# First loads on one queue, products on ones before the data, V scaled per token, four low parts on GpSimd

## The chip, the cores and the metric

One NeuronCore of a Trainium2 chip runs the whole program. The time is device microseconds of that core; the median of three runs is given. TensorE is called PE in the profile, VectorE is DVE, ScalarE is ACT, GpSimd is POOL, and SP is the queue of SyncE, which here only issues transfers.

## What is computed

The reference runs two layers and then one sparse-attention block over 512 tokens of width 1024, in float32. A layer is:

```python
h = rmsnorm(x, norm_mix_g[l])
x = x + mixer_block(h, w_in[l], ...)      # mLSTM with input/forget gates, windowed attention, two gates, w_out
h = rmsnorm(x, norm_mlp_g[l])
x = x + jnp.square(jax.nn.relu(h @ w_up[l])) @ w_down[l]
```

Of the mixer only the beginning matters here: `proj = h @ w_in` gives among others the attention's keys `ak` and values `av` (256 columns each), the eight gate columns `mi` and `mf`, and the mLSTM's input. With `rs = 1/sqrt(mean(x*x) + eps)` per token, `h` is `x * gain * rs`, so a product of `x * gain` with the weights needs only to be multiplied by `rs` per token behind it. For the gates, `log_sigmoid(mf + b)` is summed over time and a running maximum is taken.

## The kernel before

Everything is transposed: tiles are 128 channels by 512 tokens, eight of them (`k` = 0 to 7) for the width. Each float32 operand of a large product is split into a high and a low part (`fp32r`), and a product is three matmuls: high*high, low*high, high*low. A weight unit is 1024x128: SP loads its raw form (512 KB), ScalarE writes its high part in two halves (L902), GpSimd its low part in two halves (L457, `split_pairs`), TensorE takes 24 matmuls of 512 columns (L497 to L499). Units alternate between two buffers; SP loads unit n+2 when both low halves of unit n are there, and ScalarE splits a half when TensorE is through with the one before it in that buffer.

The order of work of every engine is written out as a list of steps, and each engine walks through the same list in order: `u0, h0, m1, u1` are the four quarters of a unit. The change touches the list `PRE` that stands before the main loop of each layer:

- k0 and k1: products for the attention's keys, from `hx`, the raw `x*gain` split in high (ScalarE, L997) and low (VectorE, L1509).
- norm: ScalarE squares the tiles (L993), VectorE adds them up in `ssq` (L1501, L1504), TensorE multiplies by ones (L509), ScalarE takes Ln and Exp into `rs` (L1003, L1005). In layer 0 this stands inside unit k1, ahead of its last quarter.
- gates: one more product of 24 matmuls with the gate weights (L524 to L526), in layer 0 loaded at the start and split by ScalarE (L1050) and VectorE (L1549). VectorE then makes the gate rows, 4x512 each (L1584 to L1599; `grows_done` when they are done).
- v0 and v1: products for the values; VectorE multiplies by `rs` on the way out (`vtmp`, L1401), TensorE transposes them (`TK`, L513), and ScalarE copies the result to `vtok` (L1120, L1121).
- tables (layer 0 only, behind v0): small products for the position biases, copied out by ScalarE and stored.
- gatesT: 16 small products that transpose the gate rows (L607). It needs `grows_done` and both transposing banks, which come free when ScalarE has copied the second `TK`.
- hT: VectorE writes `nt = x*gain*rs` (`tile`, L1521, three buffers), ScalarE its high part (`hi_parts`, L1037), VectorE its low part (`tile_lo`, L1515). The first unit of the loop, conv 0, reads hT one k after the other, and its first matmul starts the loop.

On ScalarE and VectorE these pieces are interleaved by hand in the order of the code, so one waiting instruction holds all behind it. In layer 0 the first loads are issued by two queues: SP issues the gains, x tile 0, weight unit 0, x tiles 2, 4, 6, unit 1 and five constants; ScalarE issues x tiles 1, 3, 5, 7, the gate weights and four tables before it loads its activation table (L987).

Of the kernel before, what the change touches and what calls it, by code (L numbers as in the profile page):

```python
# [30 lines left out]
P = 128  # L31
# [72 lines left out]
PRE_TAIL = unit("v", 0) + unit("v", 1) + [("TK", 0), ("TK", 1), ("gatesT",)]  # L104
PRE_FIRST = unit("k", 0) + unit("k", 1)[:3] + [("norm_",)] + unit("k", 1)[3:] + [("gates",)] + PRE_TAIL
# [34 lines left out]
def product_count(half, k):  # L140
# [8 lines left out]
         "CT": ["T"], "TO": ["T"], "norm_": ["O1"]}  # L149
# [81 lines left out]
def two_layers_and_nsa(nc, w_all, wg_all, vec_it, vec_l, vec_n, ident_in, tri_in, onehot_w, onehot_n,  # L231
                       tab_w, tab_n, late_in, x_in, w1_in, w2_in, pos_in, scr_w, scr_n, out):
    ctx = ExitStack()
    with ctx:
# [30 lines left out]
        late = new("late", [P, 1])  # L265
        st = new("st", [P, 12, 16])
# [127 lines left out]
        nt_ready, nhi_done = sem("nt_ready"), sem("norm_hi_done")  # L394
        h_ready, hx_hi_done, hx_ready = sem("h_ready"), sem("h_raw_hi_done"), sem("h_raw_ready")
# [26 lines left out]
        def _(sp):  # L422
# [26 lines left out]
        def _(pool):  # L449
# [11 lines left out]
            split_pairs(UNITS // 2, 0)  # L461
# [18 lines left out]
        def _(pe):  # L480
# [22 lines left out]
            def norm_sum(count, total=None):  # L503

                use = step_uses(w, ("norm_",))[0]
                pe.wait_ge(o_free[1], use.m + 1)
                pe.wait_ge(sq_used, count)
                total = ssq[:, :] if total is None else total
                nc.tensor.matmul(ps[:, 7, :], ones[:, :], total, start=True, stop=True).then_inc(o_ready[1], 1)  # L509
# [6 lines left out]
            def gate_gemm(I, use, gw, h, waits=None):  # L516
# [3 lines left out]
                for k in range(KT):  # L520
# [5 lines left out]
                    last = nc.tensor.matmul(ps[:, 7, :], wl, h[0][:, k, :], start=False, stop=(k == KT - 1))  # L526
                last.then_inc(o_ready[1], 1)
# [49 lines left out]
            pe.wait_ge(cst_done, 1)  # L577

            for l in range(DEPTH):
                for s in PRE[l]:  # L580
                    if s[0] == "norm_":
                        norm_sum(squares(l))
                        continue
# [9 lines left out]
                    elif s[0] == "TK":  # L593
# [3 lines left out]
                        heads4(4 + us[0].b, lambda t: vtmp[:, s[1], t * P:(t + 1) * P], t_ready[us[0].b])  # L597
                    elif s[0] == "gates":
                        gate_gemm(l, us[0], gw, hx)
# [12 lines left out]
                with w.loop(pe, NG, per(LOOP)) as it:  # L612
# [3 lines left out]
                    for s in LOOP:  # L616
# [3 lines left out]
                        if s[0] in UNIT_STEPS:  # L620
                            first = s[1:] == ("conv", 0)
                            quarter(s, cur["u"], *hT, waits=(lambda k: (h_ready, l * KT + k + 1)) if first else None)
# [94 lines left out]
            for s in NPRE:  # L717
# [15 lines left out]
                elif s[0] == "ngates":  # L733
                    gate_gemm(DEPTH, us[0], gwn, hT, waits=lambda k: (h_ready, DEPTH * KT + k + 1))
# [146 lines left out]
        def _(act):  # L881
# [33 lines left out]
            def store(s, u):  # L915
# [13 lines left out]
                elif kind == "v" and cur["layer"]:  # L929
                    pass  # L930
# [68 lines left out]
            def norm():  # L999

                use = w.use("O1")
                act.wait_ge(o_ready[1], use.m + 1)
                nc.scalar.activation(rs[:, :], ps[:, 7, :], ACT.Ln, bias=EPS).then_inc(o_free[1], 1)  # L1003
                act.wait_ge(o_free[1], use.m + 2)
# [73 lines left out]
            ln_exp()  # L1078
# [11 lines left out]
            gate_weights_hi(0, gw_raw, gw)  # L1090

            for l in range(DEPTH):
                cur["layer"], cur["l"] = True, l
                restart()
                for s in PRE[l]:
                    if s[0] == "norm_":
                        norm()
                        continue
                    us = take(s)
                    if s[0] in UNIT_STEPS:  # L1100
# [14 lines left out]
                        elif s == ("h0", "v", 1) and l > 0:  # L1115
                            hi_parts(l, (4,))
                    elif s[0] == "TK":
                        act.wait_ge(t_ready[us[0].b], us[0].m + 1)
                        tk = ps[:, 4 + us[0].b, :].rearrange("p (t d) -> p t d", t=TT)
                        link(nc.scalar.activation(vtok[:, 2 * s[1], :, :], tk[:, :, 0:DH], ACT.Copy))  # L1120
                        nc.scalar.activation(vtok[:, 2 * s[1] + 1, :, :], tk[:, :, DH:P], ACT.Copy)\  # L1121
                            .then_inc(t_free[us[0].b], 1)
                        if s[1] == 0 and l == 0:
                            hi_parts(l, (3,))
                        elif s[1] == 1 and l > 0:
                            hi_parts(l, (5,))
                    elif s[0] == "gates":
# [4 lines left out]
                        hi_parts(l, (2,))  # L1132
                    elif s[0] == "gatesT":

                        act.wait_ge(grows_done, l + 1)
# [6 lines left out]
                        hi_parts(l, range(4 if l == 0 else 6, KT))  # L1142
# [3 lines left out]
                act.wait_ge(h_ready, (l + 1) * KT)  # L1146
# [891 lines left out]
```

## Time and profile before

| | us |
|---|---|
| median of 3 runs (2329.92 to 2331.26) | 2329.93 |
| profiled execution | 2331.21 |
| its span, first to last instruction | 2329.0 |
| TensorE busy | 2273.5 (98%) |
| VectorE / ScalarE / GpSimd busy | 919.0 / 975.8 / 885.4 |
| mean granted TensorE clock | 0.992 |

Busy time of TensorE includes matmuls that wait for the array behind each other, so 98% means that it hardly ever stands still, not that it is at its peak. The granted clock is 1.00 for 2.4 GHz and 0.50 for 1.2 GHz.

### The profile page before, as it was taken

The page shows a single profiled execution, that of the slowest core. Times are in us where ns is not written, and L with a number is a line of the kernel's source. Part 1 is how long each engine was busy: PE and PEld are TensorE (multiplying, and loading weights), DVE is VectorE, ACT ScalarE, POOL GpSimd, SP SyncE. Part 2 cuts the span into 40 slices and gives each one's busy share as a digit, 9 for nine tenths or more (in the row PEclk, how much of TensorE's full clock was granted, in tenths as well). Part 3 has the DMA queues.
Part 4 walks back from the last instruction along what each step waited for, and adds up shares of the span by engine and source line. Part 5 has one row for each costly group of instructions (what it writes and reads, how often), then busy time and mean ns, then how long its engine had stood idle before and what let it go on. Part 6 is the DMA issues. An engine that isn't in the chain of part 4 may idle for free.

```text
span 2329.0 us, 35784 instructions
## 1 busy us (share of the span) xinstructions
PE 2273.5 (98%) x11383; PEld 1900.6 (82%) x11383; DVE 919.0 (39%) x1915; ACT 975.8 (42%) x2068; POOL 885.4 (38%) x676
## 2 busy tenths in 40 slices
PE   7999999999999999999999999999999999999997
PEld 5888888788888888888888788888888878888886
DVE  7344343423232235343343424232235525555453
ACT  5445455434232234455454434232235235444453
POOL 3332333445444444333323344544454231221213
PEclk9999999999999999999999999999999999999999
DMA  3221222222222222212212223222222321211112
GB/s 125 82 82 63 81 73 71 74 98 101 99 100 94 97 97 81 91 64 81 81 63 81 73 90 108 100 91 99 99 91 98 130 82 37 70 58 43 63 36 82
DMA packets 59945, 193.84 MB, mean 83 GB/s; under 512 B 6782, under 2 KB 13487, under 8 KB 59504
## 3 DMA queue, kind: packets, MB, share of 16 engines
q1 hardware_dynamic: 51552, 177.48, 22.4%
q10 hardware_dynamic: 8336, 15.60, 1.9%
q8 instruction: 36, 0.59, 0.1%
q14 instruction: 21, 0.17, 0.0%
HBM read 190.89 MB, written 2.16 MB: 83 GB/s over the span
## 4 chain that ended last, share of the span: by engine, by line
PE 92%; DVE 5%; ACT 2%; issue 1%; ACTq 0%; DVEq 0%
PE ps L497 25%; PE ps L499 25%; PE ps L498 25%; PE ps L559 5%; PE ps L539 3%; PE ps L547 3%; PE ps L658 1%; PE ps L513 1%; PE ps L646 1%; PE ps L763 1%; PE ps L824 1%; DVE nt L1521 0%; PE ps L813 0%; PE ps L636 0%; DVE sz L1453 0%
## 5 line engine op out<-in xcount | busy, mean ns | idle before, releaser
L457 POOL TENSOR_TENSOR w_lo<-w_raw,w_hi 128x512 fp32r<-128x512 f32 x664 | 879.3, 1327 | 1430.0 <-ACT w_hi L902 1426.2
L497 PE MATMUL ps<-hT_hi,w_hi 128*128 128x512 f32 x1600 | 652.0, 407 | 2.5 <-DVE x2v L1413 2.0
L499 PE MATMUL ps<-hT_hi,w_lo 128*128 128x512 f32 x1600 | 628.3, 393 | 0.0
L498 PE MATMUL ps<-hT_lo,w_hi 128*128 128x512 f32 x1600 | 627.0, 392 | 0.0
L902 ACT ACTIVATE w_hi<-w_raw 128x512 fp32r<-128x512 f32 x664 | 411.4, 626 | 473.8 <-PE ps L499 441.4
L497 PEld LDWEIGHTS ps<-hT_hi,w_hi 128*128 128x128 f32 x1600 | 303.1, 189 | 65.9 <-issue 8.5
L499 PEld LDWEIGHTS ps<-hT_hi,w_lo 128*128 128x128 f32 x1600 | 302.5, 189 | 66.2
L498 PEld LDWEIGHTS ps<-hT_lo,w_hi 128*128 128x128 f32 x1600 | 303.7, 190 | 55.9 <-issue 0.5
L497 PE MATMUL ps<-u_hi,w_hi 128*128 128x512 f32 x512 | 199.2, 389 | 0.0
L498 PE MATMUL ps<-u_lo,w_hi 128*128 128x512 f32 x512 | 199.2, 389 | 0.0
L499 PE MATMUL ps<-u_hi,w_lo 128*128 128x512 f32 x512 | 199.2, 389 | 0.0
L1487 DVE TENSOR_TENSOR x<-x,ps 128x512 f32<-128x512 f32 x64 | 44.0, 687 | 257.2 <-PE ps L499 257.2
L1460 DVE SCALAR_TENSOR_TENSOR e_buf<-ps,rs 128x512 f32<-128x512 f32 x64 | 44.3, 692 | 208.7 <-PE ps L499 208.7
L953 ACT ACTIVATE u_hi<-e_buf 128x512 fp32r<-128x512 f32 x64 | 40.5, 632 | 173.0 <-DVE e_buf L1460 173.0
L497 PEld LDWEIGHTS ps<-u_hi,w_hi 128*128 128x128 f32 x512 | 96.1, 188 | 20.0
L498 PEld LDWEIGHTS ps<-u_lo,w_hi 128*128 128x128 f32 x512 | 96.1, 188 | 20.0
L499 PEld LDWEIGHTS ps<-u_hi,w_lo 128*128 128x128 f32 x512 | 96.1, 188 | 19.8
L1059 ACT ACTIVATE Pn<-Ln,st 128x128 f32<-128x128 f32 (+3 forms) x128 | 71.8, 561 | 70.3 <-DVE st L1564 68.7
L1059 ACT ACTIVATE Pb<-L,st 128x256 f32<-128x256 f32 (+1 forms) x128 | 61.4, 480 | 74.4 <-DVE st L1564 73.4
L1423 DVE SCALAR_TENSOR_TENSOR aq<-ps,aq 64x512 fp32r<-64x512 f32 x32 | 22.0, 689 | 154.5 <-ACT aq L927 153.9
L1564 DVE CUSTOM_DVE_ANT_0 Ln<-ps,biasn 128x128 f32<-128x128 f32 (+3 forms) x128 | 62.7, 490 | 43.4 <-DVEq L1370 40.9
L1564 DVE CUSTOM_DVE_ANT_0 L<-ps,bias,st 128x256 f32<-128x256 f32 (+1 forms) x128 | 56.2, 448 | 52.1 <-DVEq L1370 51.3
(305 smaller groups left out, 3303.6 us busy)
## 6 DMA issues: line engine op xcount, KB each, us to landing
w_raw<-w_all SPq DMA_DIRECT2D x332, 512.0 KB, 3.2
bias<-scr_w ACTq DMA_DIRECT2D x8, 512.0 KB, 3.5
biasn<-scr_n ACTq DMA_DIRECT2D x4, 1024.0 KB, 5.2
w1k<-w_in ACTq DMA_DIRECT2D x2, 1024.0 KB, 7.5
w1v<-w_in ACTq DMA_DIRECT2D x1, 2048.0 KB, 13.7
out<-x SPq DMA_DIRECT2D x16, 128.0 KB, 1.8
x<-x_in SPq DMA_DIRECT2D x4, 256.0 KB, 6.4
x<-x_in ACTq DMA_DIRECT2D x4, 256.0 KB, 5.7
```

The lines of the kernel that those rows point to most:

```text
L457: nc.gpsimd.tensor_tensor(w_lo[:, h, :], raw[:, h // 2, (h % 2) * HALF:(h % 2 + 1) * HALF], w_hi[:, h, :].bitcast(F32), ALU.subtract).then ...
L497: nc.tensor.matmul(ps[:, p, :], wh, hi[:, kk, :], start=(kk == 0), stop=False)
L498: nc.tensor.matmul(ps[:, p, :], wh, lo[:, kk, :], start=False, stop=False)
L499: last = nc.tensor.matmul(ps[:, p, :], wl, hi[:, kk, :], start=False, stop=(kk == KT - 1))
L539: last = nc.tensor.matmul(ps[:, 2 + us[0].b, 0:nk * P], q[:, hd, qt * P:(qt + 1) * P], kk[i][:, k0 * P:(qt + 1) * P], start=(i == 0), stop ...
L547: last = nc.tensor.transpose(ps[:, 4 + us[0].b, c * P:(c + 1) * P], pb[:, j % 3, c * P:(c + 1) * P], ident[:, :])
L559: last = nc.tensor.matmul(ps[:, 6 + ob, (qt % 2) * 256 + hd * DH:(qt % 2) * 256 + (hd + 1) * DH], pt[:, j % 3, c * P:(c + 1) * P], vv[:, k ...
L902: nc.scalar.activation(w_hi[:, 2 * p + h, :], raw[:, p, h * HALF:(h + 1) * HALF], ACT.Copy)\
L1059: nc.scalar.activation(Pbuf[:, j % 3, 0:n], Lbuf[:, j % 2, 0:n], ACT.Exp, scale=-1.0, bias=st[:, 0, j:j + 1], accum_out=st[:, 1, j:j + 1]) ...
L1460: V.scalar_tensor_tensor(e_buf[:, e.b, :], g, 0.0, rs[:, :], ALU.max, ALU.mult).then_inc(g_free[u.b], 1)
L1487: V.tensor_tensor(x[:, n, :], x[:, n, :], g, ALU.add).then_inc(g_free[u.b], 1)
L1564: V.tensor_tensor_reduce(out=Lbuf[:, j % 2, 0:n], in0=ps[:, 2 + b_, 0:n], in1=reverse(bias_t, j % GH, n), scale=1.0, scalar=first, op0=ALU ...
```

## The change

- SP issues all first loads: x tiles 1 to 7 in order, unit 1, the gate weights, the five constants, the four tables. ScalarE issues none of them and loads its activation table first.
- TensorE starts with 12 products ones*ones of 128 columns, whose result nobody reads.
- The order of layer 0's beginning: the gate weights are split after the sixth square; the product with ones that makes the norm sum is put inside the gate product, behind its third k, in the other bank (`norm0`); the memsets of two gate rows go to the very start.
- V: ScalarE copies the product to `vtmp` unscaled. A new step `rsT` transposes `rs` (four transposes), ScalarE takes a column of it, `rstok`, and applies it as scale in the copy behind the transposes: four copies of 128x128 in place of two of 128x256, in both layers.
- In layer 0 GpSimd makes the low parts of hT for k = 0 to 3 (`POOL_LO`), behind the weight units 0 to 3 and ahead of unit 4, with a semaphore of its own (`h_pool`); counts on `h_ready` are less by four (`h_count`).
- VectorE's and ScalarE's pieces in layer 0's beginning are interleaved anew.

```diff
-PRE_TAIL = unit("v", 0) + unit("v", 1) + [("TK", 0), ("TK", 1), ("gatesT",)]
-PRE_FIRST = unit("k", 0) + unit("k", 1)[:3] + [("norm_",)] + unit("k", 1)[3:] + [("gates",)] + PRE_TAIL
+PRE_TAIL = unit("v", 0) + unit("v", 1) + [("rsT",), ("TK", 0), ("TK", 1), ("gatesT",)]
+PRE_FIRST = unit("k", 0) + unit("k", 1)[:3] + [("norm0",)] + unit("k", 1)[3:] + [("gates",)] + PRE_TAIL
...
+POOL_LO = 4
+def h_count(n, k):
+    return n * KT + k + 1 - POOL_LO
...
-            for k in range(2, KT, 2):
+            for k in range(1, KT):
                 nc.sync.dma_start(x[:, k, :], x_in[k * P:(k + 1) * P, :]).then_inc(x_landed[k], 16)
             nc.sync.dma_start(raw[:, 1, :], w_all[1]).then_inc(raw_in[1], 16)
+            nc.sync.dma_start(gw_raw[:, :], wg_all[0]).then_inc(gw_in, 16)
...
+            for dst, src in ((oh_w[:, :], onehot_w), (tabw[:, :], tab_w), (oh_n[:, :], onehot_n), (tabn[:, :], tab_n)):
+                nc.sync.dma_start(dst, src).then_inc(tab_in, 16)
...
-            split_pairs(UNITS // 2, 0)
+            split_pairs(2, 0)
+            for k in range(POOL_LO):
+                pool.wait_ge(nhi_done, k + 1)
+                nc.gpsimd.tensor_tensor(hT[1][:, k, :], nt[:, k % 3, :], hT[0][:, k, :].bitcast(F32), ALU.subtract)\
+                    .then_inc(h_pool, 1)
+            split_pairs(UNITS // 2 - 2, 2)
...
+                    if k == 2 and between is not None:
+                        between()
...
+            for i in range(12):
+                nc.tensor.matmul(ps[:, 5, 0:P], ones[:, :], ones[:, :], start=True, stop=True)
...
+                    elif s[0] == "rsT":
+                        pe.wait_ge(o_free[0], us[0].m + 1)
+                        pe.wait_ge(rs_ready, 2 * l + 1)
+                        heads4(6, lambda t: rs[:, t * P:(t + 1) * P], o_ready[0])
...
-                elif kind == "v" and cur["layer"]:
-                    pass
...
+            ln_exp()
...
-            for k in range(1, KT, 2):
-                nc.scalar.dma_start(x[:, k, :], x_in[k * P:(k + 1) * P, :]).then_inc(x_landed[k], 16)
-            gate_weights(0, gw_raw)
-            for dst, src in ((oh_w[:, :], onehot_w), (tabw[:, :], tab_w), (oh_n[:, :], onehot_n), (tabn[:, :], tab_n)):
-                nc.scalar.dma_start(dst, src).then_inc(tab_in, 16)
...
-                        tk = ps[:, 4 + us[0].b, :].rearrange("p (t d) -> p t d", t=TT)
-                        link(nc.scalar.activation(vtok[:, 2 * s[1], :, :], tk[:, :, 0:DH], ACT.Copy))
-                        nc.scalar.activation(vtok[:, 2 * s[1] + 1, :, :], tk[:, :, DH:P], ACT.Copy)\
-                            .then_inc(t_free[us[0].b], 1)
+                        tk = ps[:, 4 + us[0].b, :].rearrange("p (t g d) -> p t g d", t=TT, g=2)
+                        for t in range(TT):
+                            last = nc.scalar.activation(vtok[:, 2 * s[1]:2 * s[1] + 2, t, :], tk[:, t, :, :], ACT.Copy,
+                                                        scale=rstok[:, t:t + 1])
+                        last.then_inc(t_free[us[0].b], 1)
+                        if l == 0:
+                            hi_parts(l, (5 + s[1],))
...
-                        hi_parts(l, (2,))
+                        hi_parts(l, (2, 3) if l == 0 else (2,))
...
-                elif kind == "v" and cur["layer"]:
-                    product(u)
-                    V.tensor_tensor(vtmp[:, n, :], g, rs[:, :], ALU.mult).then_inc(g_free[u.b], 1)
...
                 if l == 0:
                     store(("u1", "k", 1), cur["k", 1])
+                    tile(l, 0, rs[:, :])
+                    tile(l, 1, rs[:, :])
+                    gate_rows_in(pre["gates",][0])
+                    tile(l, 2, rs[:, :])
+                    tile(l, 3, rs[:, :])
+                    gate_rows()
+                    tile(l, 4, rs[:, :])
+                    gate_rows_scan()
+                    tile_lo(l, 4)
+                    tile(l, 5, rs[:, :])
+                    gate_rows_sum()
+                    tile_lo(l, 5)
+                    tile(l, 6, rs[:, :])
+                    tile(l, 7, rs[:, :])
+                    tile_lo(l, 6)
+                    tile_lo(l, 7)
```

## Rows read from the trace of the kernel before

**Rows 1.** The page: busy time by engine; the chain that ended last, by engine.

```profile
PE 2273.5 (98%) x11383; PEld 1900.6 (82%) x11383; DVE 919.0 (39%) x1915; ACT 975.8 (42%) x2068; POOL 885.4 (38%) x676
PE 92%; DVE 5%; ACT 2%; issue 1%; ACTq 0%; DVEq 0%
```

**Rows 2.** Waits of TensorE, 0 to 60 us: total, times, longest.

```profile
PE ps L497 <- POOL w_lo L457: 10.2, 1, 10.2
PE ps L513 <- DVE vtmp L1401: 3.6, 1, 3.6
```

**Rows 3.** Windows: busy by engine, PEclk (granted clock), DMA share, GB/s.

```profile
8.00:9.00 1.00, 0.00 (x0) 0.00 (x0) 0.75 (x1) 1.00 (x2) 0.41 (x1) 1.00 1.06 408
48.00:50.00 2.00, 0.83 (x4) 0.72 (x4) 1.02 (x2) 0.00 (x0) 0.00 (x0) 0.50 0.72 260
58.00:60.00 2.00, 2.00 (x9) 1.56 (x9) 1.56 (x6) 0.60 (x1) 0.00 (x0) 0.96 0.00 0
934.00:936.00 2.00, 1.89 (x15) 1.92 (x15) 2.00 (x2) 1.14 (x3) 0.90 (x1) 0.85 0.24 94
```

**Rows 4.** ScalarE's timeline, 0 to 25 us: start, duration, instruction.

```profile
1.48 1.90 ACTq L1073 DMA_DIRECT2D x<-x_in  x4
5.97 1.28 ACT L987 ACT_TABLE_LOAD   x1 [5.97 <-issue]
9.55 3.77 ACT L997 ACTIVATE hx_hi<-x,vl 128x512 fp32r<-128x512 f32 x6
13.24 0.63 ACT L902 ACTIVATE w_hi<-w_raw 128x512 fp32r<-128x512 f32 x1
22.39 1.04 ACT L1050 ACTIVATE gw_hi<-gw_raw 128x1024 fp32r<-128x1024 f32 x1
```

**Rows 5.** The load of x tile 0 (L425): issue to landing.

```profile
DMA to landing us min/median/max: 2.7/2.7/2.7
```

**Rows 6.** VectorE's timeline, 8 to 50 us.

```profile
8.11 0.75 DVE L1509 SCALAR_TENSOR_TENSOR hx_lo<-x,vl,hx_hi 128x512 fp32r<-128x512 f32 x1 [7.10 <-ACT hx_hi L997]
10.46 1.78 DVE L1509 SCALAR_TENSOR_TENSOR hx_lo<-x,vl,hx_hi 128x512 fp32r<-128x512 f32 x1
17.03 6.38 DVE L1504 TENSOR_TENSOR ssq<-ssq,sq 128x512 f32<-128x512 f32 x7
26.32 2.80 DVE L1397 TENSOR_TENSOR kdup<-ps,rs 64x512 f32<-64x512 f32 x4
38.52 1.58 DVE L1594 SCALAR_TENSOR_TENSOR grow<-grow,vl 4x512 f32<-4x512 f32 x1
43.56 1.60 DVE L1599 TENSOR_TENSOR grow<-grow 4x512 f32<-4x512 f32 x1
48.34 0.68 DVE L1401 TENSOR_TENSOR vtmp<-ps,rs 128x512 f32<-128x512 f32 x1
```

**Rows 7.** GpSimd's timeline, 8 to 42 us.

```profile
8.59 3.10 POOL L457 TENSOR_TENSOR w_lo<-w_raw,w_hi 128x512 fp32r<-128x512 f32 x2 [8.14 <-ACT w_hi L902]
37.65 3.61 POOL L457 TENSOR_TENSOR w_lo<-w_raw,w_hi 128x512 fp32r<-128x512 f32 x2 [7.59 <-ACT w_hi L902]
```

**Rows 8.** TensorE's timeline in layer 0.

```profile
23.56 1.10 PE L509 MATMUL ps<-ssq,ones 128*128 128x512 f32 x2 [1.37 <-DVE ssq L1504]
45.00 0.60 PE L513 MATMUL ps<-ident,vtmp 128*128 128x128 f32 x4
50.19 3.57 PE L607 MATMUL ps<-ident,grow 4*128 4x4 f32 x16
53.69 0.80 PE L497 MATMUL ps<-hT_hi,w_hi 128*128 128x512 f32 x1
```

**Rows 9.** TensorE and ScalarE at the end of layer 1's beginning.

```profile
931.77 0.60 PE L513 MATMUL ps<-ident,vtmp 128*128 128x128 f32 x4
933.18 0.36 ACT L1120 ACTIVATE vtok<-ps 128x256 f32<-128x256 f32 x1
936.41 0.80 PE L497 MATMUL ps<-hT_hi,w_hi 128*128 128x512 f32 x1
```

More of the change, by code:

```diff
@@ L265, in two_layers_and_nsa @@
         late = new("late", [P, 1])
+        rstok = new("rstok", [P, TT])
         st = new("st", [P, 12, 16])
@@ L501, in quarter, with norm_sum @@
                     last.then_inc(used, 1)
-            def norm_sum(count, total=None):
-                use = step_uses(w, ("norm_",))[0]
-                pe.wait_ge(o_free[1], use.m + 1)
+            def norm_sum(count, total=None, step="norm_"):
+                use, ob = step_uses(w, (step,))[0], int(step == "norm_")
+                pe.wait_ge(o_free[ob], use.m + 1)
                 pe.wait_ge(sq_used, count)
                 total = ssq[:, :] if total is None else total
-                nc.tensor.matmul(ps[:, 7, :], ones[:, :], total, start=True, stop=True).then_inc(o_ready[1], 1)
+                nc.tensor.matmul(ps[:, 6 + ob, :], ones[:, :], total, start=True, stop=True).then_inc(o_ready[ob], 1)
             def heads4(dst_bank, src, ready):
@@ L514, in heads4, with gate_gemm @@
                 last.then_inc(ready, 1)
-            def gate_gemm(I, use, gw, h, waits=None):
+            def gate_gemm(I, use, gw, h, waits=None, between=None):
                 pe.wait_ge(gwlo_done, I + 1)
@@ L582, in _ @@
                         norm_sum(squares(l))
+                        continue
+                    if s[0] == "norm0":
                         continue
@@ L621, in _ @@
                             first = s[1:] == ("conv", 0)
-                            quarter(s, cur["u"], *hT, waits=(lambda k: (h_ready, l * KT + k + 1)) if first else None)
+                            quarter(s, cur["u"], *hT, waits=(lambda k: (h_pool, k + 1) if l == 0 and k < POOL_LO else
+                                                             (h_ready, h_count(l, k))) if first else None)
                             if s[0:2] == ("u1", "conv"):
@@ L997, in raw_hi, with norm @@
                 nc.scalar.activation(dst[:, k, :], x[:, k, :], ACT.Copy, scale=gain).then_inc(hx_hi_done, 1)
[L999 to L1004, printed above, removed]
+            def norm(ob=1):
+                use = w.use(f"O{ob}")
+                act.wait_ge(o_ready[ob], use.m + 1)
+                nc.scalar.activation(rs[:, :], ps[:, 6 + ob, :], ACT.Ln, bias=EPS).then_inc(o_free[ob], 1)
+                act.wait_ge(o_free[ob], use.m + 2)
                 nc.scalar.activation(rs[:, :], rs[:, :], ACT.Exp, scale=-0.5).then_inc(rs_ready, 1)
@@ L1095, in _ @@
                 for s in PRE[l]:
-                    if s[0] == "norm_":
-                        norm()
+                    if s[0] in ("norm_", "norm0"):
+                        norm(ob=int(s[0] == "norm_"))
                         continue
@@ L1114, in _ @@
                             tables_out()
-                        elif s == ("h0", "v", 1) and l > 0:
+                        elif s == ("h0", "v", 1):
                             hi_parts(l, (4,))
@@ L1141, in _ @@
                                              ACT.Exp, scale=-1.0).then_inc(t_free[t_.b], 1)
-                        hi_parts(l, range(4 if l == 0 else 6, KT))
+                        if l > 0:
+                            hi_parts(l, (6, 7))
                 for n in range(2):
@@ L1624, in _ @@
                     store(("u1", "k", 1), cur["k", 1])
-                tile(l, 0, rs[:, :])
-                tile(l, 1, rs[:, :])
-                tile_lo(l, 0)
-                tile_lo(l, 1)
-                gate_rows_in(pre["gates",][0])
-                tile(l, 2, rs[:, :])
-                gate_rows()
-                tile_lo(l, 2)
-                if l == 0:
-                    store(("u1", "v", 0), cur["v", 0])
-                else:
-                    store(("u1", "k", 1), cur["k", 1])
@@ new lines, in _ @@
+                    tile_lo(l, 6)
+                    tile_lo(l, 7)
+                else:
+                    tile(l, 0, rs[:, :])
+                    tile(l, 1, rs[:, :])
+                    tile_lo(l, 0)
+                    tile_lo(l, 1)
+                    gate_rows_in(pre["gates",][0])
+                    tile(l, 2, rs[:, :])
+                    gate_rows()
+                    tile_lo(l, 2)
+                    store(("u1", "k", 1), cur["k", 1])
+                    gate_rows_scan()
+                    gate_rows_sum()
+                    tile(l, 3, rs[:, :])
+                    tile_lo(l, 3)
+                    tile(l, 4, rs[:, :])
+                    tile_lo(l, 4)
+                    tile(l, 5, rs[:, :])
+                    tile(l, 6, rs[:, :])
+                    tile_lo(l, 5)
+                    tile(l, 7, rs[:, :])
+                    tile_lo(l, 6)
+                    tile_lo(l, 7)
```

60 lines of the change are left out of this document (29 added, 31 removed), and 1 row of the table TAKES.

## The prediction, made before the result was known

> **What bounds the kernel now.** First the page: TensorE is busy 98% of the span and the chain that ended last is TensorE for 92% [rows 1]. So a gain can come only from places where TensorE stands still or runs slow, and the diff touches one: the beginning of each layer. Next the waits of TensorE there: 10.2 us until the first low weights, 3.6 us for `vtmp` of v1 [rows 2], and 1.4 us ahead of the product with ones [rows 8]. Third the clock: from about 48 to 58 us it is 0.50, that is 1.2 GHz, after TensorE stood still from 45.6 to 49.2, and then everything, the first matmuls of the loop too, takes twice as long [rows 3, 8]. Layer 0's loop starts at 53.69, and this one number sums up what its beginning costs [rows 8]; layer 1's starts at 936.41, 4.6 us after the end of v1 [rows 9].
>
> **The start.** ScalarE issues nine loads from 1.48 to 5.94 and only then loads its table (1.28 us), so its first high part is at 7.27 [rows 4]. After the change the table is in by 2.8, and x tile 0 lands at 1.20 + 2.7 = 3.9 [rows 5]. From there the transfers lead: they run at about 0.40 MB per us with all engines busy [rows 3]. In SP's order gains, x0, unit 0, x1 to x7 are 2.64 MB. From about 2.9 us that is 9.5, and 0.4 for the landing: x7 is there at 9.9, its high part is made at 11.0, against 13.3 now (9.55 + 3.77) [rows 4]. SP needs some 0.47 us an issue (read off ScalarE's, 1.90 for four [rows 4]), so x7 is issued at 5 and waits for bandwidth, not for the queue. Unit 1 is 0.52 MB behind: 11.2, and its split goes from 13.24 to 11.3. The 21 issues end at about 10.7, when SP's first loop load is not yet due. So the issues moved past cost nothing.
>
> VectorE's low parts follow. One alone takes 0.75, beside GpSimd 1.78 [rows 6, 7]: a GpSimd operation costs a VectorE operation with two SBUF inputs 1.03 us. Last low part: 11.0 + 0.75 + two such hits, about 14.0; it is now near 16.5. The square sums then take 6.9 us (16.5 to 23.41) [rows 6]. Two things are newly inserted: gw_hi on ScalarE (1.04 [rows 4]) and gw_lo on VectorE (1.4 to 1.9; together about 1.9 on this chain). 14.0 + 6.9 + 1.9 = 22.8 against 23.4: **of 2.5 us won at the start only 0.6 reach the norm**. From the product with ones to the first use of `rs` is 26.32 - 23.56 = 2.76 [rows 6, 8], so `rs` is used at 25.7.
>
> The 12 products on ones run from 1.05 to about 6.2: no row shows one of this size. The 512-column one is 1.1 us [rows 8], a quarter of it 0.28, and twice that at the low clock, so 3.3 to 6.6 us in all; I take 5.1. Data is there at 7.5. Whether the clock is then up moves the end of k0 by 1.4 at most (eight slow matmuls), and the gates wait for other things anyway: 0.
>
> **TensorE up to v1.** k0 ends with the last low part plus its three matmuls, 14.7; k1 gets its second low half at 17.8 (ScalarE splits it after the fourth square) and ends at 20.6; the gate product starts there, not at 26.4, waits 0.3 for the norm sum inside it and ends at 27.4, against 32.0. From there v0, tables and v1 are the same 13.0 us (32.0 to 45.0 [rows 8]): **v1 ends at 40.4, 4.6 earlier**.
>
> **VectorE up to the gate rows.** `grows_done` is now at 43.56 + 1.60 = 45.16, 18.8 us after the first key store [rows 6]. After the change this stretch has six tiles and one low part in place of three tiles, three low parts and one V: seven operations of 0.7 us again. But GpSimd is now in it with eight operations (four low parts, four weight halves) instead of about four that hit. Its operations cost 0.9 us each where VectorE has no gap (1.58 and 1.60 for what alone takes 0.68 [rows 6]); a PSUM-fed operation is not hit (four key stores in 2.80 beside GpSimd [rows 6]). I count five or six hits, 5.2 us, in place of 3.5, and take off the 0.7 wait for ScalarE, which the two tiles ahead now fill: 18.8 + 1.7 - 0.7 = 19.8, so 25.7 + 19.8 = **45.5: no earlier than today**. The low parts moved to GpSimd give VectorE nothing net: 0.7 saved each, 0.9 paid.
>
> The Trainium skill ("SBUF — State Buffer", section "SBUF: two separate sides") says that whoever of the two engines starts first holds the shared ports for its whole instruction and the other fully blocks. The rows show most of it (1.03 of the 1.4 to 1.5 us of a GpSimd operation). What it would give at its full size is the third case below.
>
> **The tail of layer 0.** ScalarE after v1 (40.4): a high part, `vtmp` 0.7, a split 0.6, `rstok` 0.3, then four small copies for the first TK. A 128x256 copy is 0.36 [rows 9] and a 128x512 one 0.63 (hx, rows 4), so a 128x128 one is about 0.25, four are 1.0 against 0.8 for the pair. Then a high part that needs tile 5 (about 45), then the second TK: done at 46.5. gatesT takes 3.5 us now at the low clock; its first half can run from 45.5, the second from 46.5, and ends at 48.2. The loop starts at **48.2 instead of 53.69: -5.5**. hT's last low part would be ready at about 50, needed at 48.2 + 7 x 0.68 = 53: hidden. The weights of conv 0 come behind GpSimd's four low parts, about 41.6: hidden too.
>
> **The clock.** Between 40.4 and 48.2 TensorE has only transposes and small products, so I expect it to fall to 1.2 GHz as today: in layer 1 it falls at 935.4 in such a stretch of 4.6 us though nothing stands still for long [rows 3, 9]. Today 4.4 us of the loop's matmuls are slow (53.69 to 58.1), which costs 2.1. I allow 5.1 slow us, 2.4: +0.3, with 1.2 either way.
>
> The Trainium skill ("TensorE: Matmul & The Clock Gate", section "Part 4: PE-mode transpose") says that transposes do not count as work for the clock gate. By it `rsT` cannot hold the clock up; were it otherwise, the second case below would be likelier.
>
> **Layer 1.** There the V scaling was hidden in gaps of VectorE; what is added stands in the open: four transposes (0.6, beside the wait for `vtmp`), `rstok` 0.3, 0.2 more per TK, and ScalarE now has V's copy ahead of a split and the first TK. Its first TK copy moves from 933.18 [rows 9] to about 934.1, the second TK ends at 936.1 instead of 934.6, gatesT at 937.6: **+1.2** (0.3 to 2.5).
>
> **Sum.** -5.5 + 0.3 + 1.2 = -4.0 us. The profiled execution took 2331.21 (span 2329.0 and 2.2 around it), so 2327.2; the median of the runs is 1.28 under it: **2325.9**.
>
> **The cases.**
> 1. *As summed.* VectorE's gate rows and ScalarE's copies hold back gatesT; 2325.9, own range 2323 to 2328.5. Chance 0.47.
> 2. *The ports cost little.* If GpSimd's operations fall beside PSUM-fed ones or into waits (today one at 45.9 hit nothing), the gate rows are ready by 41 to 42, and ScalarE's copies alone are left: 40.4 + 4.3 + 1.5 = 46.2, -7.5 instead of -5.5; with the shorter stretch the clock may stay up, another -2. Together with layer 1: -6.3 to -8.5, so about 2322.5. For it: four hits today is already a guess from 0.9 us bumps. Against: the work stands denser than before. Chance 0.28.
> 3. *Every GpSimd operation blocks VectorE fully.* Eight hits at 1.03: 18.8 + 4.7 = 23.5, gate rows at 49.2, loop at 51.5, so -2.2 + 0.3 + 1.2 = -0.7: 2329.2. At the whole 1.44 us of a GpSimd operation it would be +2.6: 2332.5. Chance 0.20.
> 4. *Slower: conv 0 waits for GpSimd's queue.* Its first matmul needs the low weights of unit 4, which now stand behind four low parts of hT, each of which waits for a tile of VectorE and a high part of ScalarE. The two halves take 2.8 to 3.6 us [rows 7]. If the fourth low part ends later than 50, conv 0 starts later than today; at 55 it is 58.6, +4.9, with layer 1 +6: 2336. I have that low part at 39, so VectorE would have to be 11 us late. Chance 0.05.
>
> Two runs apart by less than 0.2% (4.7 us) I call the same. Faster by more is below 2325.3: 0.20 of case 1's 0.47 and nearly all of case 2's, 0.46. Slower is above 2334.6: 0.06. The rest, 0.48, is the same. The range to hold 8 in 10 takes most of case 2 and of case 3: 2319.5 to 2331.5.
>
> **What would show it.** Right: first high part near 4 us; last raw low part near 14; gate product from about 20.6 with the product on ones inside; `grows_done` at 44 to 47; the loop's first matmul at 47 to 49.5; clock 0.50 around it; layer 1's distance from v1 to the loop 5.5 to 6 instead of 4.6. Wrong: VectorE operations of 0.7 us beside GpSimd's low parts (case 2), a wait of L497 on `w_lo` or `hT_lo` at conv 0 (case 4), k0 slow because the clock wasn't up and the gates late for it, or a difference in the main loops, which I hold to be untouched.

## The result: 15 us slower, and not where the change was made

| 4 runs each | median us | lowest to highest | ratio to before, 95% interval |
|---|---|---|---|
| before | 2329.93 | 2328.14 to 2331.26 | |
| changed | 2345.24 | 2344.66 to 2346.75 | 1.0067, 1.0050 to 1.0085 |

The profiled execution of the changed kernel took 2346.75, its span is 2344.9: 15.9 more than before. The forecast was 2325.9, with 2319.5 to 2331.5 as range. Its page answers [rows 1] like this:

```profile
PE 2296.7 (98%) x11415; PEld 1906.5 (81%) x11415; DVE 914.7 (39%) x1907; ACT 979.3 (42%) x2082; POOL 891.8 (38%) x680
PE 92%; DVE 4%; ACT 2%; issue 2%; POOL 0%; ACTq 0%; DVEq 0%; POOLq 0%
```

The chain is TensorE for 92% as before, but TensorE is busy 23.2 us longer, with 32 more matmul records: 24 of the 12 products on ones, which the trace shows as two records each, and 8 of the transposes of `rs`, four in each layer. Together they are 5.2 + 1.2 us. So some 17 us are left, and the matmuls themselves must have slowed. The beginning did not grow: TensorE's timeline in layer 0 (start, duration, instruction), against [rows 8]:

```profile
24.30 1.04 PE L527 MATMUL ps<-ssq,ones 128*128 128x512 f32 x2
41.82 0.60 PE L531 MATMUL ps<-ident,rs 128*128 128x128 f32 x4
48.60 3.57 PE L635 MATMUL ps<-ident,grow 4*128 4x4 f32 x16 [4.21 <-DVE grow L1633]
52.09 0.80 PE L515 MATMUL ps<-hT_hi,w_hi 128*128 128x512 f32 x1
```

The loop starts at 52.09 instead of 53.69. From there to layer 1's loop it is 891.6 us (to 943.67) against 882.7 before (53.69 to 936.41, [rows 8, 9]). Nine microseconds are lost in layer 0's main loops, which no line of the change touches. One 200 us window of the MLP, before and after, shows how. First the windows (busy and count by engine in the order PE, PEld, DVE, ACT, POOL, then granted clock, DMA share, GB/s), before:

```profile
600.00:800.00 200.00, 200.00 (x884) 165.68 (x883) 48.29 (x70) 55.61 (x91) 97.82 (x74) 1.00 0.29 98
```

and after:

```profile
600.00:800.00 200.00, 200.00 (x870) 162.96 (x869) 48.76 (x71) 54.81 (x90) 95.47 (x72) 1.00 0.29 97
```

Busy 100% and clock 1.00 both times, but 870 matmuls in place of 884. A matmul has two operands in SBUF: the weights (128x128), which are loaded into TensorE first, and the moving tile (128x512), which is streamed past them. Groups of that window with shapes kept apart (count | busy us, mean ns of one | idle before), before:

```profile
L497 PE MATMUL ps<-u_hi,w_hi 128*128 128x512 f32 x167 | 65.0, 389 | 0.0
L497 PE MATMUL ps<-hT_hi,w_hi 128*128 128x512 f32 x128 | 49.8, 389 | 0.0
```

and after:

```profile
L515 PE MATMUL ps<-u_hi,w_hi 128*128 128x512 f32 x161 | 63.6, 395 | 0.0
L515 PE MATMUL ps<-hT_hi,w_hi 128*128 128x512 f32 x129 | 50.2, 389 | 0.0
```

The matmuls that read `hT` are as fast as before, those that read `u` take 6 ns more. Over the whole trace, the mean time from the start of a 512-column matmul to the next (those of 215 to 260 ns), with the weight tile beside the moving one; `gw` and `gwn` are the gate weights of the layers and of the last block:

| moving tile | weights | matmuls | before ns | changed ns |
|---|---|---|---|---|
| hT (address 32896) | w | 4800 | 228.2 | 228.2 |
| u (97920, now 98048) | w | 1536 | 226.7 | 233.3 |
| y (130688, now 130816) | w | 528 | 226.8 | 233.1 |
| ha (163456, now 163584) | w | 384 | 226.7 | 233.0 |
| hx (130688, now 130816) | w | 288 | 227.9 | 232.5 |
| hx, as above | gw (moved by 128 too) | 48 | 227.3 | 227.8 |
| hT, as above | gwn (moved by 128) | 24 | 227.4 | 232.2 |

The addresses tell the slow ones from the fast ones. The change puts a new tile, `rstok` (16 bytes per partition, for which 128 are set aside), between `late` and `st`, and every tile behind it moves by 128. `x`, `hT` and the weights `w` lie ahead of it and stay. (6.6 x 1536 + 6.3 x 912 + 4.6 x 288) ns = 17.2 us. The last two rows already say what the experiments confirm: a pair is slow where one of its two tiles moved, and fast where both moved or neither.

The changed kernel's start, ScalarE's timeline, against [rows 4]:

```profile
0.74 1.28 ACT L1014 ACT_TABLE_LOAD   x1 [0.74 <-PEq L2079]
3.85 0.72 ACT L1024 ACTIVATE hx_hi<-x,vl 128x512 fp32r<-128x512 f32 x1 [1.82 <-DMA x<-x_in]
6.85 0.63 ACT L931 ACTIVATE w_hi<-w_raw 128x512 fp32r<-128x512 f32 x1 [2.28 <-DMA w_raw<-w_all]
8.64 3.77 ACT L1024 ACTIVATE hx_hi<-x,vl 128x512 fp32r<-128x512 f32 x6
```

TensorE there, and windows of the clock:

```profile
1.06 5.21 PE L599 MATMUL ps<-ones 128*128 128x128 f32 x24 [1.06 <-DVE ones L1635]
8.93 0.50 PE L515 MATMUL ps<-hx_hi,w_hi 128*128 128x512 f32 x1 [2.67 <-issue]
```

```profile
8.00:10.00 2.00, 1.07 (x3) 0.95 (x4) 1.74 (x2) 2.00 (x5) 2.00 (x2) 0.81 1.06 407
10.00:12.00 2.00, 2.00 (x6) 1.45 (x5) 2.00 (x3) 2.00 (x4) 0.52 (x1) 0.50 1.04 422
```

The products on ones end 2.7 us before there is data, and the clock falls to 1.2 GHz just as the first real matmuls run: the second starts 0.31 us behind the first, the third 0.41 behind that. VectorE's timeline up to the gate rows, against [rows 6]:

```profile
26.68 2.81 DVE L1429 TENSOR_TENSOR kdup<-ps,rs 64x512 f32<-64x512 f32 x4 [2.58 <-ACT rs L1032]
33.15 1.67 DVE L1618 SCALAR_TENSOR_TENSOR grow<-grow 4x512 f32<-4x512 f32 x1
36.89 2.23 DVE L1624 TENSOR_TENSOR_SCAN grow<-grow 4x512 f32<-4x512 f32 x1
39.15 1.61 DVE L1625 SCALAR_TENSOR_TENSOR grow<-grow,vl 4x512 f32<-4x512 f32 x1
42.39 2.28 DVE L1629 TENSOR_TENSOR_SCAN grow<-grow 4x512 f32<-4x512 f32 x1
47.87 0.67 DVE L1633 TENSOR_TENSOR grow<-grow 4x512 f32<-4x512 f32 x1
```

and GpSimd's in the same stretch, against [rows 7]:

```profile
31.55 2.73 POOL L477 TENSOR_TENSOR hT_lo<-nt,hT_hi 128x512 fp32r<-128x512 f32 x2 [3.02 <-ACT hT_hi L1064]
36.74 3.48 POOL L477 TENSOR_TENSOR hT_lo<-nt,hT_hi 128x512 fp32r<-128x512 f32 x2 [2.46 <-ACT hT_hi L1064]
40.18 7.22 POOL L470 TENSOR_TENSOR w_lo<-w_raw,w_hi 128x512 fp32r<-128x512 f32 x4
```

Every VectorE operation with two SBUF inputs that starts while GpSimd is at work takes 0.9 to 1.1 us more: the scans 2.23 and 2.28, one alone 1.21. The ends tell why. Whether such an operation starts early or late in GpSimd's, it ends 0.54 or 0.55 us behind GpSimd's end, and a scan 1.07 or 1.08. Three of the seven:

| VectorE: start, end | GpSimd's operation: start, end | VectorE's end behind GpSimd's |
|---|---|---|
| 33.15, 34.82 | 32.80, 34.28 | 0.54 |
| 36.89, 39.12 (scan) | 36.74, 38.04 | 1.08 |
| 39.15, 40.76 | 37.99, 40.22 | 0.55 |

So VectorE stands until GpSimd has finished, and what it loses is the rest of GpSimd's operation. GpSimd in turn takes 1.7 to 2.2 us for what takes 1.28 alone when VectorE has no gaps. The gate rows are done at 48.54, TensorE waits 4.2 us for them, and the tail is a late one, near the third case. The end of layer 1's beginning, ScalarE and TensorE, against [rows 9]:

```profile
940.47 2.17 ACT L1143 ACTIVATE vtok<-ps,rstok 128x128 f32<-128x128 f32 x8
```

```profile
938.77 0.60 PE L531 MATMUL ps<-ident,rs 128*128 128x128 f32 x4
941.75 1.99 PE L635 MATMUL ps<-ident,grow 4*128 4x4 f32 x16 [1.13 <-ACT vtok L1143]
943.67 0.50 PE L515 MATMUL ps<-hT_hi,w_hi 128*128 128x512 f32 x1
```

### The profile page after: what moved, and what is told of

It is laid out like the page before. It is cut to its first block, busy times and chain, and to the rows that moved or that the text cites. A ratio compares the mean times of both kernels' runs of the same rounds, so it can differ in the third digit from the quotient of the medians.

```text
span 2344.9 us, 35559 instructions
## 1 busy us (share of the span) xinstructions
PE 2296.7 (98%) x11415; PEld 1906.5 (81%) x11415; DVE 914.7 (39%) x1907; ACT 979.3 (42%) x2082; POOL 891.8 (38%) x680
## 4 chain that ended last, share of the span: by engine, by line
PE 92%; DVE 4%; ACT 2%; issue 2%; POOL 0%; ACTq 0%; DVEq 0%; POOLq 0%
PE ps L515 25%; PE ps L517 25%; PE ps L516 25%; PE ps L579 5%; PE ps L559 3%; PE ps L567 3%; PE ps L687 1%; PE ps L531 1%; PE ps L675 1%; PE ps L792 1%; PE ps L853 1%; DVE nt L1552 1%; PE ps L842 0%; PE ps L665 0%; DVE sz L1482 0%
## 5 line engine op out<-in xcount | busy, mean ns | idle before, releaser
L515 PEld LDWEIGHTS ps<-u_hi,w_hi 128*128 128x128 f32 x512 | 96.1, 188 | 23.2
## 6 DMA issues: line engine op xcount, KB each, us to landing
w1v<-w_in ACTq DMA_DIRECT2D x1, 2048.0 KB, 12.4
```

Of the source, the lines that this page charges most:

```text
L515: nc.tensor.matmul(ps[:, p, :], wh, hi[:, kk, :], start=(kk == 0), stop=False)
```

## The experiments

The main theory is that 128 bytes in front of the moving tiles cost 16 to 17 us and the change itself is worth about its -1.6 us at the loop's start. The rival is that the changed order of instructions slows the matmuls. Kernels called `b_` start from the kernel before, `a_` from the changed one. "Before" in the ratios is the kernel before, run on the same chip.

**a_noshift: the whole change without the shift.**

```diff
-        rstok = new("rstok", [P, TT])
+        rstok = new("rstok", [P, TT], at=[top[0] - 64])
```

> The changed kernel with rstok put into the unused part of the 128 bytes of the tile 'late', so that every tile behind it stands again at the address it had before. Main theory (the 128 bytes that rstok adds shift the tiles u, y, ha and hx, and a matmul that reads one of them starts 6 to 7 ns later than before; 2,700 of them, 16 us): 2345.2 - 16 = about 2329, with a start-to-start distance of 226.7 ns again for ps<-u matmuls. Rival (the distance grows from the changed instruction stream, not from addresses): 2345 and 233 ns.

2328.01 us (10 runs, 2326.02 to 2332.03), ratio 1.0002 (0.9992 to 1.0011). The window is back at 884 matmuls, `u` at the old duration:

```profile
L515 PE MATMUL ps<-u_hi,w_hi 128*128 128x512 f32 x167 | 65.0, 389 | 0.0
```

One tile's address makes 17.2 us (2345.24 - 2328.01; by the two ratios, 1.0067 and 1.0002, 15 us), and nothing of the instruction stream. It also shows what the rest of the change is worth in the median: nothing that can be told from zero, although its loop starts at 51.02.

**b_pad128: the shift without the change.**

```diff
         late = new("late", [P, 1])
+        top[0] += 128
```

> The kernel before with nothing changed but 128 unused bytes ahead of the tile st. Main theory: 2330 + 16 to 17 = 2346.5, ps<-u at 233 ns, ps<-hT unchanged at 227.6. Rival (instruction stream): 2330.

2348.32 us (4 runs), ratio 1.0086 (1.0069 to 1.0103). `u` slow, `hT` not:

```profile
L498 PE MATMUL ps<-u_hi,w_hi 128*128 128x512 f32 x160 | 63.2, 395 | 0.0
L498 PE MATMUL ps<-hT_hi,w_hi 128*128 128x512 f32 x130 | 50.6, 389 | 0.0
```

**b_all128: every tile 128 further.**

```diff
-        base = 16512
+        base = 16512 + 128
```

> The kernel before with all its tiles 128 bytes further, the weights too. If it is the moving tile's own address (a start at a multiple of 256 bytes is slow, 128 past one is fast): ps<-hT matmuls slow down as well, 4,500 x 6.5 ns = 29 us more, in all 2330 + 46 = 2376. If it is the distance between moving tile and weights (both 128 past a multiple of 256 is fast, one of each is slow): everything as before, 2330.

2328.41 us (10 runs), ratio 0.9995 (0.9985 to 1.0005). All fast:

```profile
L497 PE MATMUL ps<-u_hi,w_hi 128*128 128x512 f32 x166 | 64.6, 389 | 0.0
L497 PE MATMUL ps<-hT_hi,w_hi 128*128 128x512 f32 x128 | 49.8, 389 | 0.0
```

So it is not the moving tile's own address.

**b_weights128: the weights and all behind them 128 further, x and hT not.**

```diff
+        top[0] += 128
         raw = new("w_raw", [P, 2, KT * P])
```

> The kernel before with 128 unused bytes between hT and the raw weights: x and hT stay, the weights and everything behind (u, y, ha, hx) move by 128. By the moving tile's own address: u, y, ha, hx slow, hT fast, 2346.5 as with the pad ahead of st. By the distance between moving tile and weights: u, y, ha, hx fast again, hT and hm slow, 4,900 x 6.5 ns: 2330 + 32 = 2362.

2354.61 us (4 runs), ratio 1.0118 (1.0101 to 1.0135). Now `hT` is the slow one:

```profile
L498 PE MATMUL ps<-u_hi,w_hi 128*128 128x512 f32 x156 | 60.7, 389 | 0.0
L498 PE MATMUL ps<-hT_hi,w_hi 128*128 128x512 f32 x134 | 52.9, 395 | 0.0
```

`u` was moved just as in b_pad128 and is fast, because the weights moved along. What counts is the distance between the moving tile and the weights. One rival is left: ScalarE and GpSimd write weight tiles all through the loop, and the clash could be with them. It is not: in the changed kernel's trace 349 of the `u` matmuls ran while neither of the two worked on a weight tile, and they took 233.1 ns, the others 233.3. The size is 25.7 us, not 32: over the whole trace `hT` went from 228.2 to 232.7, 4.5 ns and not 6.5.

**b_pad256 and b_pad64 (twice): which distances.** The same line as b_pad128 with 256 and with 64.

> The kernel before with 256 unused bytes ahead of the tile st. Theory (only the distance between moving tile and weights modulo 256 bytes counts): no change, 2329, ps<-u at 226.7 ns. Rival (modulo 512 or 1024 counts; so far all fast pairs were a multiple of 512 apart): slow like 128, 2346 to 2348, or half of it.

2328.48 us, ratio 0.9994 (0.9983 to 1.0004), `u` at 226.7 ns. A distance of 256 bytes, though no multiple of 512, is fast.

> The kernel before with 64 unused bytes ahead of the tile st instead of 128. Theory (a matmul is fast when moving tile and weights lie a multiple of 256 bytes apart; each other distance slows it): u, y, ha, hx slow by some 6 ns as at 128, about 2346. Rival (only a distance of 128 bytes past a multiple of 256 is slow, half of it does nothing): 2330. Third: it is slower still, because a matmul then straddles more.

2335.71 us, ratio 1.0027 (1.0017 to 1.0036), but the profiled execution took 2350.26 at a granted clock of 0.95 in its windows (0.941 in the mean), with `u` at 232.6.

> The kernel before with 64 unused bytes ahead of the tile st, a second time: the first gave 2335.7 as median, yet its profiled execution took 2350.3 with a granted clock of 0.949 where others have 1.00, and 232.6 ns for ps<-u. Theory (a distance of 64 bytes costs less than one of 128, and the profiled execution was an exception): profiled execution near the median, 2334 to 2338, ps<-u at about 229 ns. Rival (64 costs as much as 128): ps<-u at 233 ns and 2346.

2335.09 us, ratio 1.0030 (1.0019 to 1.0041), profiled execution 2334.42. The three kinds of matmul now differ: high*high 231.7, low*high 225.9, high*low 229.2 ns, where all had 226 to 227. So 64 bytes cost a third of what 128 cost (ratios 1.0027 and 1.0030 against 1.0086). Why the first profiled execution was slower stays open; its granted clock of 0.95 was seen in no other trace, and its `hT` matmuls were as fast as ever (228.2 ns).

**a_no_ones: without the products on ones** (from a_noshift).

```diff
-            for i in range(12):
-                nc.tensor.matmul(ps[:, 5, 0:P], ones[:, :], ones[:, :], start=True, stop=True)
```

> The changed kernel with rstok out of the way and without the 12 products on ones. Theory: they buy nothing, because in the profile they end at 6.3 us, the first product with data starts at 8.9, the clock is back at 1.2 GHz from 9.3 to 12.7 and the norm sum waits for VectorE anyway: within 0.5 us of the kernel with them (2328), product on ones of the norm sum at 24 to 24.5. Rival (they keep the clock up for the start): norm sum and loop start later by 1 to 1.7 us, 2329.5.

2328.18 us, ratio 0.9999 (0.9990 to 1.0009): the same. Its TensorE runs the first data products at the low clock, 0.43 us apart (the distance is the sign here, the windows show 1.00), where a_noshift's are 0.23 apart:

```profile
8.44 0.77 PE L515 MATMUL ps<-hx_hi,w_hi 128*128 128x512 f32 x1 [8.44 <-POOL w_lo L470]
9.00 0.63 PE L516 MATMUL ps<-hx_lo,w_hi 128*128 128x512 f32 x1
9.43 0.63 PE L517 MATMUL ps<-hx_hi,w_lo 128*128 128x512 f32 x1
```

The norm sum's product is at 24.34 and the loop starts at 52.11, against 23.21 and 51.02 in a_noshift. But these executions differ in two things: ScalarE splits the first weight unit at 6.20 here and at 5.77 in a_noshift, by when it landed. And the changed kernel, with the products, but with that split at 6.85 and the clock lost, has 24.30 and 52.09. So the 1.1 us in the traces can't be put down to the products alone. A part can: here VectorE has its square sum ready at 23.45 and TensorE takes it 0.9 later, while in a_dve_low below, which has the products and the sum at 23.51, TensorE takes it at 23.71. That is some 0.6 us in one trace each; the medians show nothing.

**b_loads: SP issues all first loads, nothing else** (from the kernel before).

```diff
-            for k in range(2, KT, 2):
+            for k in range(1, KT):
                 nc.sync.dma_start(x[:, k, :], x_in[k * P:(k + 1) * P, :]).then_inc(x_landed[k], 16)
...
+            nc.sync.dma_start(gw_raw[:, :], wg_all[0]).then_inc(gw_in, 16)
...
-            for k in range(1, KT, 2):
-                nc.scalar.dma_start(x[:, k, :], x_in[k * P:(k + 1) * P, :]).then_inc(x_landed[k], 16)
-            gate_weights(0, gw_raw)
```

> The kernel before with one part of the change alone: SP issues all first loads and ScalarE loads its table first. Theory (start and norm come earlier, but VectorE's chain and ScalarE's order hold the tail): first high part at 3.9, last raw low part at 15.3, product on ones of the norm sum 1 to 1.5 us earlier than 23.56, loop start 1 to 1.5 us earlier than 53.69, 2327.5 to 2328.5. Rival (nothing arrives at the loop): 53.7 and 2329.

2325.38 us (10 runs), ratio 0.9988 (0.9978 to 0.9997): a little more than either theory gave.

```profile
21.97 1.10 PE L512 MATMUL ps<-ssq,ones 128*128 128x512 f32 x2 [1.37 <-DVE ssq L1501]
47.59 0.63 PE L516 MATMUL ps<-ident,vtmp 128*128 128x128 f32 x4 [3.57 <-DVE vtmp L1398]
48.15 2.82 PE L610 MATMUL ps<-ident,grow 4*128 4x4 f32 x16
50.91 0.80 PE L500 MATMUL ps<-hT_hi,w_hi 128*128 128x512 f32 x1
```

The norm comes 1.6 us earlier, the loop 2.8. That is as early as in a_noshift (51.02): **this one part carries all that the change wins in layer 0**, and the rest together wins nothing on top. What holds the loop back is another thing here: the gate rows are done at 43.56, and TensorE waits 3.6 us for `vtmp` of v1, as in the kernel before.

**a_dve_low: the four low parts back on VectorE** (from a_noshift).

```diff
-POOL_LO = 4
+POOL_LO = 0
...
                     tile(l, 1, rs[:, :])
+                    tile_lo(l, 0)
+                    tile_lo(l, 1)
...
                     gate_rows()
+                    tile_lo(l, 2)
+                    tile_lo(l, 3)
```

> The changed kernel with rstok out of the way and all low parts of hT on VectorE again (two behind tile 1, two behind the gate rows' first three steps); GpSimd makes only weights. Theory (a GpSimd operation costs VectorE 0.9 to 1.0 us here, more than the 0.7 it saves): gate rows done 0.5 to 2 us earlier than 47.4, loop start 49 to 50.5 instead of 51.0, 2327. Rival (GpSimd's help is worth 0.7 a piece): 2.7 us later, loop start 53.7, 2330.7.

2327.59 us, ratio 0.9998 (0.9989 to 1.0008); gate rows done at 47.80 against 47.45, loop start 51.35 against 51.02. Neither theory's number. Even the 0.3 us are not GpSimd's: v1 ends 0.5 later here (41.01 against 40.52), and the gate rows take 21.7 us from the first key store on against 21.8. Its help is worth nothing that the traces show, and it costs nothing.

**a_rows_first: the gate rows ahead of the tiles, and ScalarE's high parts 2 to 7 behind the V copies** (from a_dve_low).

```diff
                     store(("u1", "k", 1), cur["k", 1])
+                    gate_rows_in(pre["gates",][0])
                     tile(l, 0, rs[:, :])
                     tile(l, 1, rs[:, :])
+                    gate_rows()
+                    gate_rows_scan()
+                    gate_rows_sum()
                     tile_lo(l, 0)
                     tile_lo(l, 1)
...
-                            if l == 0:
-                                hi_parts(l, (0, 1))
...
-                        hi_parts(l, (2, 3) if l == 0 else (2,))
+                        hi_parts(l, (0, 1) if l == 0 else (2,))
...
                         if l == 0:
-                            hi_parts(l, (7,))
+                            hi_parts(l, (2, 3))
...
-                            hi_parts(l, (6, 7))
+                        hi_parts(l, range(4 if l == 0 else 6, KT))
```

> As the one before, and in layer 0 VectorE makes the gate rows ahead of all tiles but two, ScalarE takes the high parts 2 to 7 behind the V copies. Theory (the gate rows alone hold gatesT back by 4.2 us in the changed kernel, and TensorE has nothing else to do): rows done at 40 to 41, gatesT bound by ScalarE's second V copy, loop start 46 to 47.5, so 3.5 to 5 us under the changed kernel without the shift, 2324. Rival (the high parts now come too late for the first unit, or the clock falls all the same and eats it): waits of L515 on hT_lo at conv 0, less than 2 us won.

2321.68 us (6 runs, 2319.52 to 2324.58), ratio 0.9970 (0.9957 to 0.9982): 0.3% and clear of the noise, **below both kernels**. VectorE and TensorE:

```profile
36.08 2.20 DVE L1623 TENSOR_TENSOR_SCAN grow<-grow 4x512 f32<-4x512 f32 x1
38.32 0.68 DVE L1627 TENSOR_TENSOR grow<-grow 4x512 f32<-4x512 f32 x1
```

```profile
41.12 1.14 PE L531 MATMUL ps<-ident,vtmp 128*128 128x128 f32 x8
43.38 1.99 PE L635 MATMUL ps<-ident,grow 4*128 4x4 f32 x16 [1.12 <-ACT vtok L1141]
45.29 0.50 PE L515 MATMUL ps<-hT_hi,w_hi 128*128 128x512 f32 x1
```

The gate rows are done at 39.0 instead of 47.8 (13.2 us behind the first key store and not 21.7), gatesT waits for ScalarE's second V copy only, and the loop starts at 45.29, 6.1 earlier than in a_dve_low; 0.3 of that is an earlier end of v1. The clock stays at 2.4 GHz from 42 to 60 us. A wait of 0.4 us for `hT_lo` in conv 0 is the price. Two orders were changed together, VectorE's and ScalarE's, and no run tells what each is worth. The traces suggest that both were needed: in the changed kernel ScalarE, in its order, waits for tile 5 until 47.98 and has the second V copy only at 49.64.

**a_tk_early: rsT inside unit v1, in layer 1 the first TK too** (from a_rows_first; in layer 1 ScalarE's high parts 4 and 5 and VectorE's low part 4 move too).

```diff
+TAIL_FIRST = unit("v", 0) + unit("v", 1)[:3] + [("rsT",)] + unit("v", 1)[3:] + [("TK", 0), ("TK", 1), ("gatesT",)]
+TAIL_LATER = unit("v", 0) + unit("v", 1)[:2] + [("rsT",), ("TK", 0)] + unit("v", 1)[2:] + [("TK", 1), ("gatesT",)]
```

> As the kernel with the gate rows first (2321.7), and rsT stands inside unit v1 in both layers; in layer 1 the first TK does too, and ScalarE's high parts 4 and 5 come behind the V copies. Theory (in layer 1 4.9 us lie between v1 and the loop, 2.2 of them ScalarE's eight copies): layer 1 wins 1 to 1.5 us, layer 0 0.4, and where the shorter stretch keeps the clock up up to 3 us more: 2317 to 2320.5. Rival (the copies only move, and gatesT waits for the same thing): 2321.7.

2322.38 us (10 runs), ratio 0.9971 (0.9961 to 0.9981): no better than a_rows_first. The layers' loops start at 45.50 and 928.32 (45.29 and 927.44 there). In layer 0 the clock falls behind the loop's start in this execution (granted 0.59 and 0.56 from 46 to 50 us, 1.00 in a_rows_first). In layer 1 gatesT starts 0.1 us sooner, at 925.43, but runs in two parts (1.05 us from there and 1.66 from 926.73), and the clock falls at 927.0; in a_rows_first it is one part of 1.99, and the clock falls at 928.0, with the loop already running.

## Why the prediction was wrong

**The step that failed** is the last clause of the prediction: "a difference in the main loops, which I hold to be untouched". The instructions there are untouched, the addresses of what they read are not. `rstok` was read as a tile to be filled and scaled with, never as 128 bytes ahead of large tiles that TensorE reads. Sizes of tiles and the order of their allocation stand in the diff; the addresses follow by adding up, and nobody added them up. What the runs showed in its place: every matmul whose moving tile had moved against its weights takes 233 ns and not 227. The price is 15 to 17 us when it is taken away (a_noshift) and 19 when it is put in alone (b_pad128, 2348.32 against 2328.93); that it is the distance is shown by b_all128 and b_weights128. It makes the sign of the result.

No row of the trace of before could have given the price, since all its pairs were fast.

**Point by point**, the beginning as forecast (measured in the changed kernel, and in a_noshift, where the first weight unit landed sooner):

- *ScalarE's first high part at 3.9*: 3.85, right. *Last high part at 11.0*: 12.4. ScalarE could split weight unit 0 only from 6.85, not from the 5.3 that the sum's rate of transfer gives, and, in order, waited 2.3 us for it with x tiles 1 and later already due. In a_noshift, a_rows_first and a_no_ones the same split is at 5.77, 5.96 and 6.20: this landing moves by 1.1 us from one execution to another, and the sum had it as fixed.
- *Last raw low part at 14.0*: 15.4. *The norm 0.6 earlier*: its product ran at 24.30, 0.7 **later** than before. The sum's own step from the last low part to the norm was right (8.8 us, measured 8.9 from 15.4 to 24.3); the 1.4 us are the start's. The split of the gate weights, moved ahead of the last squares, costs the 1.9 us in it that were reckoned with; b_loads, which leaves it behind them, has the product at 21.97.
- *The products on ones are worth nothing*: right in the medians; some 0.6 us at the norm in the trace of a_no_ones. The clock at the first data products was lost in the changed kernel and held in a_noshift.
- *v1 ends at 40.4*: 41.8, and 40.5 in a_noshift. Right in a_noshift; in the changed kernel the start's 1.4 us are in it.
- *Gate rows at 45.5*: **48.5**. One of the 3.0 us comes from the start (`rs` used at 26.7, not 25.7). The other two are the mis-sized term of layer 0: the stretch took 21.9 us, not 19.8. I counted five or six hits of GpSimd at 0.9, 5.2 us; the trace shows eight operations lengthened, by 0.35 to 1.07 each and 7.2 in all (the scans 2.23 and 2.28 among them). The mechanism was the third case's, which had 0.20: every GpSimd operation blocks. Its stretch, 23.5, was too long by almost as much, and its 49.2 comes near the measured 48.5 partly by luck, because the start was late.
- *The Trainium skill's lock rule* ("SBUF — State Buffer", section "SBUF: two separate sides") holds here as it stands: the ends above show VectorE waiting for GpSimd's end each time. What I priced by it was wrong. VectorE loses only what is left of GpSimd's operation when its own begins, so eight whole operations (11.5 us) are too many; measured are 7.2. The trace of before has the same 0.55 us: VectorE's operation at 38.52 ends at 40.10, GpSimd's at 39.55.
- *The low parts on GpSimd give nothing net*: right, by a_dve_low.
- *The loop at 48.2*: 52.1 (a_noshift 51.0); -1.6 (-2.7) and not -5.5. Of the 3.9 us 3.0 are the gate rows. The rest was a slip in the sum: gatesT, 3.5 us long at the low clock, cannot start at 45.5 and end at 48.2; it would have ended at 49.0. Measured are 48.60 to 52.09. *The clock falls all the same*: right, 1.2 GHz from 46.8 to 57.
- *Layer 1 +1.2*: from the end of v1 to the loop 4.9 us (a_noshift 5.3) against 4.64: +0.3 to +0.7. The eight small copies take 2.17 together, near the 2.0 estimated, but the rest was put too dear.
- *Transposes and the clock*: no run tells whether the transposes of `rs` count for it.

Without the shift the forecast would have been 2.1 us too low (2325.9 against 2328.0) and in its range: the true answer for the rest of the change was "the same". That it would have been so near is in part luck, since layer 0 won less than forecast and layer 1 lost less.

The traces and the medians answer different questions here. Single executions of the kernel before spread over 2325 to 2334, the fastest at a mean granted clock of 0.995 and the slowest at 0.990, so changes of 2 us were read from the start of the loop in the traces, and only the ratios decide on the medians.

## What to carry to other kernels

When a diff allocates anything, write down the address of each tile behind it, and keep moving tiles and weights a multiple of 256 bytes apart; put small new tiles last or into padding. When TensorE waits for one chain of an in-order engine, move that chain ahead before handing pieces of its work to an engine that blocks it: the order, VectorE's and ScalarE's together, was worth 5.7 us here, the hand-over nothing. And try the parts alone: one of six parts carried all the gain in layer 0.

## What the runs showed of the hardware

- A 128x128 by 512-column fp32r matmul takes 226.7 ns from start to start when moving tile and weights lie 0 or 256 bytes apart modulo 512 (b_all128, b_pad256), 232.6 to 233.3 at 128 or 384 (b_pad128, b_weights128), and 226 to 232 at 64 (b_pad64_again). That both move together does nothing. The Trainium skill ("SBUF — State Buffer", section "A bandwidth-pool intuition that's wrong (but worth ruling out)") gives TensorE a second, independent read port for loading weights. By it alone the distance would not matter; the runs say that it does, by 2.9%. In these traces TensorE loads the next weights (PEld) while a tile streams, which fits this, but no run took one of the two away, so the mechanism is argued and not shown.
- A VectorE operation with two SBUF inputs that starts while GpSimd's runs ends 0.54 or 0.55 us behind GpSimd's end, a scan 1.07 or 1.08, in the changed kernel 0.9 to 1.07 us later than alone, on 4 partitions as much as on 128. GpSimd's 1.28 us become 1.7 to 2.2 where VectorE has no gaps. One that starts 1.16 us into a GpSimd operation of 1.26 is not lengthened (0.69 at 47.07 in the kernel before). Operations with one input from PSUM are left alone (four key stores in 2.81 us, two of them beside GpSimd).
- The records of the products on ones start 0.21 us apart, and 0.11 apart where the clock has risen: in the changed kernel the last of them, in a_tk_early the last four. In both the clock was lost again around the pause before the first data products (2.7 us, granted 0.81 and then 0.50; 2.0 us, 0.70 and 0.50). In a_noshift, a_rows_first and a_dve_low all records are 0.21 apart, the clock is up when the data comes after 1.3, 1.5 and 1.8 us, and it stays. These runs don't separate the length of the pause from the moment of the rise.
